# Gated rows and two convolution inputs as split products, with remainders made by GpSimd

## The reference

```python
def hybrid_layer(x, g_mix, w_in, w_conv_a, gmlp_ln_g, gmlp_ln_b, w_s, b_s, ...):
    h = rmsnorm(x, g_mix)
    z = h @ w_in
    (a_b, a_c, a_h, g_u, g_v, q, k, v, q_idx, k_idx, w_idx, d_a, d_g) = jnp.split(z, cuts, axis=-1)
    y_a = short_conv_mixer(a_b, a_c, a_h, w_conv_a)      # b * causal_dwconv(c * h, w)
    y_b = gmlp_mixer(g_u, g_v, gmlp_ln_g, gmlp_ln_b, w_s, b_s)
    y_c = dsa_mixer(q, k, v, q_idx, k_idx, w_idx)        # indexer, top 64, softmax
    y_d = conformer_conv_mixer(d_a, d_g, w_conf, b_conf, conf_ln_g, conf_ln_b)
    x = x + jnp.concatenate([y_a, y_b, y_c, y_d], axis=-1) @ w_out
    hf = rmsnorm(x, g_ffn)
    return x + (jax.nn.silu(hf @ w_gate) * (hf @ w_up)) @ w_down
```

## Time and profile before

| | us |
|---|---|
| median of 3 runs (range) | 1025.69 (1025.5 to 1029.27) |
| the profiled execution, its time | 1025.64 |
| the profiled execution, its span | 1023.9 |
| PE busy in the span | 972.1 (95%) |
| DVE busy | 635.2 (62%) |
| ACT busy | 378.5 (37%) |
| POOL busy | 66.9 (7%) |

### The profile page before, as it was taken

One profiled execution on the slowest core, in us unless ns is written; L12 is line 12 of the kernel. 1 busy time (PEld: TensorE's weight loads), 2 busy tenths in 40 slices (PEclk: granted clock), 3 DMA queues, 4 the chain that ended last, 5 costly groups with the idle time before them and its releaser, 6 DMA issues.

```text
span 1023.9 us, 14620 instructions
## 1 busy us (share of the span) xinstructions
PE 972.1 (95%) x5826; PEld 755.8 (74%) x5826; DVE 635.2 (62%) x1249; ACT 378.5 (37%) x589; POOL 66.9 (7%) x111
## 2 busy tenths in 40 slices
PE   8999999999999999999999999999898899999953
PEld 7868889999999868889999997966787354444321
DVE  6998589898755898689898746543656701111102
ACT  6343543434443143544444345434814231111101
POOL 0002000000000002000100001000631000000000
PEclk9999999999999999999999999999989999999988
DMA  9625367575545424378787663122079889999993
GB/s 364 286 83 205 118 252 291 211 307 212 210 156 202 168 83 193 112 313 319 298 348 283 229 245 129 72 83 83 0 319 380 342 356 383 422 420 411 405 421 125
DMA packets 30295, 251.87 MB, mean 246 GB/s; under 512 B 3872, under 2 KB 4128, under 8 KB 5920
## 3 DMA queue, kind: packets, MB, share of 16 engines
q1 hardware_dynamic: 30240, 251.14, 61.7%
HBM read 250.08 MB, written 1.05 MB: 245 GB/s over the span
## 4 chain that ended last, share of the span: by engine, by line
PE 86%; DMA 5%; DVE 4%; ACT 3%; issue 1%; POOL 1%; SPq 0%; DVEq 0%; POOLq 0%
PE bank L730 18%; PE bank L731 17%; PE bank L732 17%; PE bank L1368 10%; PE bank L721 9%; PE bank L1384 4%; DMA m<-in_experts 4%; PE bank L1321 1%; PE bank L1339 1%; PE bank L750 1%; PE bank L1130 1%; DMA kwi_w<-in_w_in 1%; PE bank L790 1%; PE bank L738 1%; ACT m L1697 1%
## 5 line engine op out<-in xcount | busy, mean ns | idle before, releaser
L730 PE MATMUL bank<-h_h,fw_h 128*128 128x256 f32 x704 | 195.2, 277 | 2.2 <-issue 2.2
L732 PE MATMUL bank<-h_h,fw_l 128*128 128x256 f32 x704 | 195.0, 277 | 0.0
L731 PE MATMUL bank<-h_l,fw_h 128*128 128x256 f32 x704 | 194.9, 277 | 0.0
L2094 DVE TENSOR_TENSOR fw_l<-blocks_w,fw_h 128x1024 fp32r<-128x1024 f32 x132 | 156.1, 1218 | 3.5 <-ACT fw_h L1564 3.4
L730 PEld LDWEIGHTS bank<-h_h,fw_h 128*128 128x128 f32 x704 | 132.2, 188 | 4.7 <-issue 3.0
L731 PEld LDWEIGHTS bank<-h_l,fw_h 128*128 128x128 f32 x704 | 132.3, 188 | 1.7
L732 PEld LDWEIGHTS bank<-h_h,fw_l 128*128 128x128 f32 x704 | 132.3, 188 | 0.0
L1564 ACT ACTIVATE fw_h<-blocks_w 128x1024 fp32r<-128x1024 f32 x132 | 129.7, 1050 | 4.8 <-DMA blocks_w<-in_ffn 4.8
L1587 ACT ACTIVATE acts<-bank 128x256 f32<-128x256 f32 x44 | 16.9, 385 | 200.5 <-PE bank L732 200.5
L2137 DVE SCALAR_TENSOR_TENSOR m<-m,scratch 128x512 f32<-128x512 f32 x128 | 90.0, 744 | 0.0
L1368 PE MATMUL bank<-m,scratch 128*64 128x512 f32 (+2 forms) x272 | 78.8, 610 | 8.9 <-DMA blocks_w<-in_experts 6.4
(11 more groups left out here) (405 smaller groups left out, 1810.4 us busy)
## 6 DMA issues: line engine op xcount, KB each, us to landing
m<-in_experts SPq DMA_DIRECT2D x51, 1024.0 KB, 11.3
blocks_w<-in_ffn SPq DMA_DIRECT2D x22, 2048.0 KB, 7.9
blocks_w<-in_experts SPq DMA_DIRECT2D x42, 1024.0 KB, 10.0
m<-in_w_ada SPq DMA_DIRECT2D x24, 1024.0 KB, 8.6
m<-in_w_in SPq DMA_DIRECT2D x11, 2048.0 KB, 9.5
blocks_w<-in_ffn SPq DMA_DIRECT2D x22, 1024.0 KB, 4.9
m<-in_w_out SPq DMA_DIRECT2D x6, 2048.0 KB, 7.5
blocks_w<-in_w_in SPq DMA_DIRECT2D x2, 2048.0 KB, 19.3
```

The costliest lines, as they stand in the source:

```text
L730: pe.matmul(out_, xh, wh, start=first and i == 0, stop=False, skip_group_check=True)
L731: pe.matmul(out_, xh, wl, start=False, stop=False, skip_group_check=True)
L732: ins = pe.matmul(out_, xl, wh, start=False, stop=last and i == n - 1, skip_group_check=True)
L2094: dve.tensor_tensor(fw_l[:, slot, at], blocks_w[:, slot, at], f32(fw_h[:, 1 - slot, at]), ALU.subtract)\
```

## The change

`guv`, `ac` and `ab` become split products; `ah` stays whole. ScalarE rounds the `guv` weights between its copies of vqi's two halves, into `w_l[:, 2]`, and the `abac` weights behind the score copies, into the place where qk's high part was. The remainders of both, and those of `w_out` (before in `rest_in` on VectorE), are now made by GpSimd, each in four pieces of 128x1024, in the place of the raw weights. The semaphores `mid_hi`, `mid_lo` and `out_lo` are new; `in_lo` counts 12 pieces a layer instead of 20.

```diff
@@ -405,6 +405,7 @@
         qk_h = fw_l[:, 1, 0:4096]
+        abac_h, abac_l = fw_l[:, 1, 0:4096], fw_l[:, 0, 0:4096]
...
@@ -885,14 +886,14 @@
-                pe.wait_ge(m_in[3], 16 * l + 16)
-                for t in range(NT):
-                    whole_tokens("guv", m[:, 3, :], t)
+                pe.wait_ge(mid_lo, 8 * l + 4)
+                for t in range(NT):
+                    split_tokens("guv", w_l[:, 2, :], w_l[:, 3, :], t)
                 pe.wait_ge(ah_in, 16 * l + 16)
                 whole_features("ah", blocks_w[:, 0, 4096:6144], 0)
-                pe.wait_ge(ab_in, 16 * l + 16)
-                whole_features("ac", blocks_w[:, 0, 0:4096], 256)
-                whole_features("ab", blocks_w[:, 0, 0:4096], 0)
+                pe.wait_ge(mid_lo, 8 * l + 8)
+                split_features("ac", abac_h, abac_l, 256)
+                split_features("ab", abac_h, abac_l, 0)
...
@@ -958,7 +959,7 @@
-                pe.wait_ge(in_lo, IN_SUBS * l + OUT0 + 4)
+                pe.wait_ge(out_lo, 8 * l + 4)
...
@@ -987,7 +988,7 @@
-                pe.wait_ge(in_lo, IN_SUBS * l + OUT1 + 4)
+                pe.wait_ge(out_lo, 8 * l + 8)
...
@@ -1476,6 +1477,11 @@
+                def rounded_mid(dst, src):
+                    for n in range(4):
+                        at = slice(n * 1024, (n + 1) * 1024)
+                        act.activation(dst[:, at], src[:, at], ACT.Copy).then_inc(mid_hi, 1)
+
...
@@ -1515,6 +1521,8 @@
                 vqi_copy(0)
+                act.wait_ge(m_in[3], 16 * l + 16)
+                rounded_mid(w_l[:, 2, :], m[:, 3, :])
                 vqi_copy(1)
...
@@ -1524,6 +1532,8 @@
+                act.wait_ge(ab_in, 16 * l + 16)
+                rounded_mid(abac_h, blocks_w[:, 0, 0:4096])
                 for t in range(NT):
                     res.ready(act, f"guv{t}")
...
@@ -1987,8 +1997,6 @@
-                    if r in (4, 5, 6, 7):
-                        rest_in(l, OUT0, w_l[:, 0, :], m[:, 0, :], w_l[:, 2, :], (r - 4,))
...
@@ -2070,7 +2078,6 @@
-                rest_in(l, OUT1, w_l[:, 1, :], m[:, 1, :], w_l[:, 3, :])
...
@@ -2600,14 +2607,31 @@
+                def rest_of_mid(first, low, raw, high):
+                    for n in range(4):
+                        at = slice(n * 1024, (n + 1) * 1024)
+                        pool.wait_ge(mid_hi, 8 * l + first + n + 1)
+                        pool.tensor_tensor(low[:, at], raw[:, at], f32(high[:, at]), ALU.subtract).then_inc(mid_lo, 1)
+
+                def rest_of_out(s, subs):
+                    for n in subs:
+                        at = slice(n * 1024, (n + 1) * 1024)
+                        pool.wait_ge(in_hi, IN_SUBS * l + (OUT0, OUT1)[s] + n + 1)
+                        pool.tensor_tensor(w_l[:, s, at], m[:, s, at], f32(w_l[:, 2 + s, at]), ALU.subtract).then_inc(out_lo, 1)
+
+                rest_of_mid(0, w_l[:, 3, :], m[:, 3, :], w_l[:, 2, :])
...
+                rest_of_mid(4, abac_l, blocks_w[:, 0, 0:4096], abac_h)
+                rest_of_out(0, (0, 1))
                 pool.wait_ge(var_ready, 2 * l + 1)
                 root(S, 2, bnag[:, 0:2, 1], 2, None, LN_EPS, norm_rstd)
+                rest_of_out(0, (2, 3))
...
+                rest_of_out(1, (0, 1))
                 pool.wait_ge(var_ready, 2 * l + 2)
                 root(S, 4, bnag[:, 2:4, 1], 2, None, LN_EPS, norm_rstd)
+                rest_of_out(1, (2, 3))
```

More of the change, by code:

```diff
@@ L112 @@
 TAPS_FIRST = 18
-IN_SUBS = 20
+IN_SUBS, IN_LOWS = 20, 12
 DADG, VQI, QK, OUT0, OUT1 = 0, 4, 8, 12, 16
@@ L511, in build @@
         prm_in, rows_ws_in, kwi_in, ab_in = sem("prm_in"), sem("rows_ws_in"), sem("kwi_in"), sem("ab_in")
-        ah_in = sem("ah_in")
+        ah_in, mid_hi, mid_lo, out_lo = sem("ah_in"), sem("mid_hi"), sem("mid_lo"), sem("out_lo")
         m_in = [sem(f"m{n}_in") for n in range(4)]
@@ L857, in _ @@
                 else:
-                    pe.wait_ge(in_lo, IN_SUBS * l + DADG + 4)
+                    pe.wait_ge(in_lo, IN_LOWS * l + DADG + 4)
                     split_features("dg", w_l[:, 3, :], w_l[:, 2, :], T)
                     split_features("da", w_l[:, 3, :], w_l[:, 2, :], 0)
-                pe.wait_ge(in_lo, IN_SUBS * l + VQI + 4)
+                pe.wait_ge(in_lo, IN_LOWS * l + VQI + 4)
                 for t in range(NT):
                     split_tokens("vqi", vqi_h[:, :], w_l[:, 0, :], t)
-                pe.wait_ge(in_lo, IN_SUBS * l + QK + 4)
+                pe.wait_ge(in_lo, IN_LOWS * l + QK + 4)
                 for t in range(NT):
```

## The result

The changed kernel takes **1073.46 us** (median of 4 runs, 1071.37 to 1073.77) beside 1025.6 us for the kernel before on the same chip (4 runs): a ratio of **1.0464, 95% interval 1.0444 to 1.0483**. It is slower by 48 us, 24 a layer in the mean of the two. The forecast was 1072 us with a range of 1045 to 1090. The total fits, so the question of the runs is whether each term of the sum does.

The account below looks back on a forecast made before the run. TensorE was taken as the bound, with VectorE 0.86 us behind. VectorE's +25.0 us (ready at 112.2, not 87.2) delays the projection 21.4 us; with 1.7 for the clock, 23.1 a layer, +46.2 in two: 1072 us, range 1045 to 1090.

Parts of the forecast that it names:

- TensorE, -5.2 us: TensorE's products in each layer: guv as split products saves 2.6 us, ac and ab together another 2.6 us.
- Step 1: Long-convolution taps and rotations: four guv subtractions on GpSimd hold VectorE 2.33 us each, +9.3 us.
- Step 2: Top-k: six GpSimd subtractions (four ac/ab, two output weights) hold VectorE, 2.0 us each in the mean, +12.2 us.
- Step 3: Top-k rounds 5 to 7: the output weights' next two GpSimd subtractions hold VectorE, +4.1 us.
- Step 4: Short convolution: the first two subtractions of the output weights' second half hold VectorE, +3.9 us.
- Step 5: Top-k rounds: four remainders are removed from VectorE's chain, -4.5 us.
- From the ab product to the projection: VectorE's product (0.69 us), gated sums (1.8) and mix remainder (0.7) precede the projection; TensorE's other jobs fit its wait.
- The clock: TensorE idle ahead of the projection: 3.4 us at 1.2 GHz, half lost, +1.7 us a layer, bounds 0 and 3.4.
- A: Rival: GpSimd does not hold VectorE's taps, so the kernel gets faster, 1015.3 us; chance 0.15.
- B: Rival: VectorE goes first whenever both wait, GpSimd runs only in MAX8 and match-replace, 1061 us; chance 0.12.
- C: Rival: each of 14 GpSimd subtractions ahead of the ab product holds VectorE only 0.44 us, 1022 us; chance 0.05.
- The upper end: GpSimd's queued subtractions run in a row with no tap between them: 28.8 us a layer with clock, 1083 us.

Follow-up runs that it names:

- The best version: Changed kernel with guv whole, ac and ab split, six remainders a layer on GpSimd, taps' running sum in PSUM: 1021.58 us, ratio 0.9964 to the kernel before.
- experiment 1: Changed kernel with GpSimd's 32 subtractions replaced by fills that read nothing, remainders zero: 1015.63 us, ratio 0.990 to the kernel before.
- experiment 9: Changed kernel with unread TensorE products put into its idle time ahead of the mix and a later job: 1066.25 us, ratio 1.0387 to the kernel before.
- experiment 4: Changed kernel with the long-convolution taps' running sum in PSUM instead of SBUF, GpSimd's work unchanged: 1040.92 us, ratio 1.0142 to the kernel before.

## Why the prediction was right

The decisive choice was the hold of a tap by a GpSimd row, between 0.44 and 2.33 us. The runs give 2.16 us (the maximum in the change), 1.96 in the mean of 14 rows, and 2.2 us for a rotation. It was chosen from short rows by the argument that 0.44 and 0.48 us were most of what those GpSimd instructions run when alone; that argument held. By steps:

- **TensorE, -5.2 us.** The best version shows ac and ab at -2.4 us a layer (forecast -2.6); guv takes 11.4 us in the change (56.85 to 68.27), -2.4 too. The 9.8 us of experiment 1 are 4.9 a layer. In the change this saving is hidden behind VectorE, as the prediction had it.
- **Step 1, guv, +9.3 us.** Measured: ten taps 12.62 - 4.04 = 8.6 us, thus 2.15 and not 2.33 for each. The top-k starts at 66.66 (forecast 66.6), but 0.8 us of that are loads that ended later in this execution.
- **Step 2, six in the top-k, +12.2 us.** Measured 10.9: three pairs of 4.48, 4.43 and 4.63 us, where an unheld pair takes 0.87. **Step 3** was +4.1 and is 3.8 (4.67 for a pair).
- **Step 4, the short convolution, +3.9 us.** Measured 4.2: 2.79 for 0.71 and 3.75 for 1.66.
- **Step 5, -4.5 us,** was not measured by itself. The sum, +25.0, would be 8.6 + 10.9 + 3.8 + 4.2 - 4.5 = 23.0 with these sizes. The ab product, 23.9 us after 87.2, less 0.8 for the loads, gives 23.1.
- **From the ab product to the projection, 3.2 us.** This step failed in part. The prediction said that the transposes, the mix and the logits are done in TensorE's wait, and counted VectorE's own steps alone. VectorE is through with them 2.9 us behind the ab product (113.98), but the last wait is not for it. The last job of the logits needs bank 6, which VectorE empties only behind the ab product; the transposes of the long convolution and of y_b follow, and then ScalarE's copy of y_b out of bank 0, where the projection's first sum goes. With TensorE at the full clock this takes 4.0 us (experiment 9), 0.8 more. A kernel with this job in another bank was not run.
- **The clock, +1.7 us.** This is the term that was mis-sized, and its upper bound of 3.4 was too low as well. Experiment 9 gives about 4.2 in the first layer: 1.9 us in the stretch just named and some 2.3 in the projection's first 12 products. The prediction took the length of another low stretch (3.4 us around 744 to 746); this one lasts from 92 to 122 and also covers the last logits and the transposes, which stand on the path.

So the mechanism was right, but that the total came out within 1.5 us is luck: two errors cancel. VectorE arrives 1.9 us a layer earlier than forecast, while the clock and the steps ahead of the projection take some 3.3 us more. The forecast of 23.1 a layer becomes 23.1 - 1.9 + 0.8 + 2.5 = 24.5 in the first layer; the mean of the two is 24. ScalarE's roundings were rightly taken as covered; the cost without the cover was given as 3.8 us at most, and experiments 1 and 4 show 1.5 and 1.6 us in the first layer.

Of the rivals, A (1015.3) is refuted as a forecast and confirmed as a price. B, VectorE first whenever both wait, is refuted by guv's rows: GpSimd did its four in 10.28 us, from 41.09 on, in the middle of VectorE's stream. C, the short hold, falls with the taps' maximum. The upper end, GpSimd's rows in a row, falls with 12.62 us for ten taps, in which each row of GpSimd let one tap through.

What stays open: how much of the 48 us the clock takes in all, since experiment 9 kept it up in one layer only. No version was tried with guv split and the rotations moved out of GpSimd's way.

## What to carry to other kernels

Before work goes from VectorE to GpSimd, list where the operands of VectorE's instructions lie in that stretch: if both are in SBUF, the move costs the critical engine most of the length of each GpSimd row, here 1.96 us a row (up to 2.16, where the rows take 2.45 to 2.57) for the 1.16 us saved. Taps with one operand in PSUM (a running sum is the natural one) ran free beside the same rows, and taps with two SBUF operands ran free beside a GpSimd instruction that reads nothing; then look for the next instruction in the stream that still reads two, or copies or scales from SBUF. And if a change opens a long idle time on TensorE ahead of a product-bound stage, count the low clock for all that TensorE still does on the path, not only at the stage's first products, and look which PSUM banks keep its jobs from being done in the wait.

## What the runs showed that was not expected

- An idle TensorE costs twice: of 48 us some 8 are the clock, and unread products in the idle time won that much back (1.0464 to 1.0387).
- A hold does not vanish when its victim is cured. With the taps in PSUM GpSimd's guv rows held three rotations instead, a 128x160 one for 2.52 us where it takes 0.32.
- A GpSimd fill, which reads nothing, held a VectorE copy of 128x64 for 0.85 us (1.05 and not 0.20), while the taps beside it ran free.
- A sum in PSUM costs a tap 4 ns (481 and not 477), and the kernel nothing (1.0005).
- GpSimd pays for the alternation too: 2.57 us a row beside held taps, 2.32 beside the taps in PSUM.
